# The first weights of a diffusion step's modulation ahead of the small rows, the second group in a buffer of its own, x behind the first activation

## The reference

```python
mod = (jax.nn.silu(c) @ w_mod[l] + b_mod[l])[:, None, :]      # c_ctx for the context tokens
shift1, scale1, gate1, shift2, scale2, gate2 = jnp.split(mod, 6, axis=-1)
mix, new_ctx = token_mixer(modulate(x, shift1, scale1), w_in, ...)   # attention and RG-LRU
x = layer_norm(ALPHA * x + gate1 * mix, ln1_g, ln1_b)
ff = expert_choice_ffn(modulate(x, shift2, scale2), w_router, w_gate_up, w_down)
x = layer_norm(ALPHA * x + gate2 * ff, ln2_g, ln2_b)
```

## Time and profile before

| | us |
|---|---|
| median of 3 runs | 944.03 (942.81 to 944.91) |
| the profiled execution, its own time | 944.97 |
| its span, first to last instruction | 943.20 |
| TensorE busy | 882.9 (94%) |
| VectorE busy | 774.0 (82%) |
| ScalarE busy | 576.1 (61%) |
| GpSimd busy | 160.8 (17%) |
| first modulation matmul starts | 12.88 |
| first `hmod` starts | 40.76 |

### The profile page before, as it was taken

The page is one execution under the profiler, slowest core; times in us unless marked ns, Lnnn a source line. Parts: engine busy times, 40 slices in busy tenths (PEclk is TensorE's granted clock), DMA queues, the critical chain, the costliest instruction groups (busy, mean ns, idle before and its releaser), DMA issues.

```text
span 943.2 us, 11657 instructions
## 1 busy us (share of the span) xinstructions
PE 882.9 (94%) x4643; PEld 602.8 (64%) x4643; DVE 774.0 (82%) x802; ACT 576.1 (61%) x588; POOL 160.8 (17%) x108
## 2 busy tenths in 40 slices
PE   2899999889999976999999999999999999999995
PEld 0389978356678843666666666666666666666663
DVE  2777736578779887888989989998998998998877
ACT  1344367735751343777777777777777777677653
POOL 1000300010011014203203303303302311320220
PEclk9899999999999986999999999999999999999999
DMA  8930500663048387999999999999999999999716
GB/s 281 396 129 1 207 1 1 262 162 114 1 152 314 138 322 286 362 419 386 415 393 385 417 389 392 410 396 391 401 403 387 390 409 382 384 414 388 275 15 200
DMA packets 57358, 272.81 MB, mean 289 GB/s; under 512 B 6788, under 2 KB 7032, under 8 KB 40920
## 3 DMA queue, kind: packets, MB, share of 16 engines
q1 hardware_dynamic: 48264, 242.76, 65.7%
q0 software_dynamic: 7600, 24.06, 9.2%
q10 hardware_dynamic: 1440, 5.24, 1.4%
HBM read 258.05 MB, written 14.00 MB: 288 GB/s over the span
## 4 chain that ended last, share of the span: by engine, by line
PE 85%; DMA 5%; DVE 5%; ACT 2%; issue 1%; SPq 1%; ACTq 0%; DVEq 0%
PE PS L918 24%; PE PS L920 24%; PE PS L919 24%; DMA ring<-in_w_mod 4%; PE PS L932 2%; PE PS L1081 2%; PE PS L1065 2%; PE PS L1035 1%; PE PS L1104 1%; PE PS L1223 1%; PE PS L1236 1%; DMA acc_scratch<-ysc,idx_u 1%; PE PS L1159 1%; DVE smin L1558 1%; ACT prob L721 1%
## 5 line engine op out<-in xcount | busy, mean ns | idle before, releaser
L1737 DVE TENSOR_TENSOR Wl<-wr,Wh 128x2048 fp32r<-128x2048 f32 x190 | 432.4, 2289 | 50.1 <-ACT Wh L832 50.1
L832 ACT ACTIVATE Wh<-wr 128x2048 fp32r<-128x2048 f32 x192 | 367.3, 1915 | 67.6 <-PE PS L920 67.6
L918 PE MATMUL PS<-Wh,Xh 128*80 128x512 f32 x512 | 202.4, 395 | 1.5 <-DVE Xl L1742 0.8
L920 PE MATMUL PS<-Wl,Xh 128*80 128x512 f32 x512 | 201.0, 393 | 0.0
L919 PE MATMUL PS<-Wh,Xl 128*80 128x512 f32 x512 | 200.8, 392 | 0.0
L543 POOL DMA_INDIRECT acc_scratch<-ysc,idx_u x15 | 81.2, 5410 | 418.6 <-DVE ysc L1768 418.6
L920 PEld LDWEIGHTS PS<-Wl,Xh 128*80 128x80 f32 x512 | 75.7, 148 | 42.1
L918 PEld LDWEIGHTS PS<-Wh,Xh 128*80 128x80 f32 x512 | 75.7, 148 | 41.8 <-issue 1.2
L918 PE MATMUL PS<-Wh,HTh 128*80 128x512 f32 x256 | 101.6, 397 | 0.0
L919 PEld LDWEIGHTS PS<-Wh,Xl 128*80 128x80 f32 x512 | 75.8, 148 | 39.4
L919 PE MATMUL PS<-Wh,HTl 128*80 128x512 f32 x256 | 100.4, 392 | 0.0
(11 more groups left out here) (298 smaller groups left out, 1211.4 us busy)
## 6 DMA issues: line engine op xcount, KB each, us to landing
wr<-in_w_gate_up SPq DMA_DIRECT2D x128, 1024.0 KB, 13.6
wr<-in_w_down SPq DMA_DIRECT2D x64, 1024.0 KB, 12.3
ring<-in_w_mod SPq DMA_DIRECT2D x24, 1024.0 KB, 9.0
xt<-in_x_sample ACTq DMA_DIRECT2D x8, 512.0 KB, 8.6
ring<-in_w_in SPq DMA_DIRECT2D x4, 1024.0 KB, 12.4
ring<-in_w_out SPq DMA_DIRECT2D x4, 1024.0 KB, 11.9
w_qkv<-in_w_in SPq DMA_DIRECT2D x4, 768.0 KB, 10.2
h_scratch<-h POOLq DMA_DIRECT2D x5, 512.0 KB, 5.8
```

Of the source, the lines that this page charges most:

```text
L832: act.activation(Wh[n % NWH][:], wr[s][:], ACT.Copy).then_inc(W_hi, 1)
L918: pe.matmul(out, w[0], x[0], start=first, stop=False)
L920: return pe.matmul(out, w[0], x[1], start=False, stop=last)
L1737: dve.tensor_tensor(Wl[s][:], wr[s][:], Wh[n % NWH][:].bitcast(F32), ALU.subtract).then_inc(W_lo, 1)
```

## The change

SyncE no longer issues the ten small requests: it starts with the four units of group 0, without a wait, then four requests for group 1, which go into a new buffer `w_mod1` (in the space that `Hh` and `Hl` take later) with semaphores of their own, then `w_qkv`, the router and the units of `w_in`, whose waits on `mod_used` are those of the ring's slots as before. The rows go to a tile of their own, `rows`. ScalarE issues the ten small requests, runs a Silu on a scratch element, which loads that table, waits for `nb_ok`, writes `cT`, and only then issues the five chunks of x. `x_again` is folded into `x_in` with a higher count, which changes no wait.

```diff
@block.sync
-        for r0, src in ((R_C, ...), ... (R_H0, ...)):
-            sp.dma_start(ring[r0:r0 + src.shape[0], 7, 0:P], src).then_inc(rows_in, 16)
-            if r0 == R_C:
-                sp.dma_start(consts[:], t["consts"][:, 0:P + 256]).then_inc(rows_in, 16)
...
-            if u == 3:
-                sp.wait_ge(rows_t, 1)
...
-        for u in range(8):
-            stream(u, slots(u), w_mod_v[:, 2 * (u % 4):2 * (u % 4) + 2, u // 4, :])
-            if u == 7:
-                for m in range(4):
-                    sp.dma_start(w_qkv[:, 2 * m:2 * m + 2, 0:QKV], w_in_v[:, 2 * m:2 * m + 2, 0:QKV]).then_inc(w_qkv_in[m], 16)
-                sp.dma_start(w_rt[:], rt_w).then_inc(misc_in, 16)
+        for u in range(4):
+            stream(u, slots(u), w_mod_v[:, 2 * u:2 * u + 2, 0, :])
+        for m in range(4):
+            sp.dma_start(w_mod1[:, 2 * m:2 * m + 2, :], w_mod_v[:, 2 * m:2 * m + 2, 1, :]).then_inc(mod1_in[m], 16)
+        for m in range(4):
+            sp.dma_start(w_qkv[:, 2 * m:2 * m + 2, 0:QKV], w_in_v[:, 2 * m:2 * m + 2, 0:QKV]).then_inc(w_qkv_in[m], 16)
+        sp.dma_start(w_rt[:], rt_w).then_inc(misc_in, 16)
@block.scalar
-        act.wait_ge(rows_in, 16 * 10)
+        for r0, src in ((R_C, ...), ... (R_H0, ...)):
+            act.dma_start(rows[r0:r0 + src.shape[0], :], src).then_inc(rows_in, 16)
+            if r0 == R_C:
+                act.dma_start(consts[:], t["consts"][:, 0:P + 256]).then_inc(rows_in, 16)
+
+        act.wait_ge(ct_zero, 1)
+        act.activation(table_scr[:, 1:2], epsc[:], ACT.Silu)
+        act.wait_ge(nb_ok, 1)
+        act.activation(cT[:, :, 0], cols[:, R_C:R_C + 8], ACT.Silu).then_inc(ct_ok, 1)
+        act.activation(cT[:, :, 32], cols[:, R_CTX:R_CTX + 8], ACT.Silu).then_inc(ct_ok, 1)
         for c in range(CH):
             src = x_s[:, c, :] if c < PC else t["x_prompt"][0]
             act.dma_start(xt[:, c, :], src).then_inc(x_in[c], 16)
-
-        act.wait_ge(nb_ok, 1)
-        act.wait_ge(ct_zero, 1)
-        act.activation(cT[:, :, 0], cols[:, R_C:R_C + 8], ACT.Silu).then_inc(ct_ok, 1)
-        act.activation(cT[:, :, 32], cols[:, R_CTX:R_CTX + 8], ACT.Silu).then_inc(ct_ok, 1)
         act.activation(nsp[:, 2, :], lscr[:, 0, :], ACT.Exp, scale=-1.0).then_inc(lam_e, 1)
@block.tensor
-        pe.transpose(bank(7, 0, R_END), ring[0:R_END, 7, 0:P], ident[0:R_END, 0:R_END]).then_inc(rows_t, 1)
+        pe.transpose(bank(7, 0, R_END), rows[0:R_END, :], ident[0:R_END, 0:R_END]).then_inc(rows_t, 1)
...
-                if k % 2 == 0:
+                if k % 2 == 0 and g == 1:
+                    pe.wait_ge(mod1_in[k // 2], 16)
+                elif k % 2 == 0:
                     landed_wait(pe, u0 + k // 2)
+                src = w_mod1 if g == 1 else ring
```

More of the change, by code:

```diff
@@ L186, in _build @@
     idx_u = tile("idx_u", [SL, NE], U32)
-    table_scr = tile("table_scr", [P, 1])
+    table_scr = tile("table_scr", [P, 2])
     epsc = tile("epsc", [P, 1])
@@ L214, in _build @@
     WX = [[at(f"WX{g}{h}", [P, KC, RG], Dz + 16384 * (2 * g + h), F32R) for h in range(2)] for g in range(2)]
+    w_mod1 = at("w_mod1", [P, KC, 1024], Ez)
     Hh = at("Hh", [P, KC, NT], Ez, F32R)
@@ L222, in _build @@
     Z = Fz + 19456
+    rows = at("rows", [P, P], Fz + 2048)
     m_rowA = [at("m_rowA0", [P, H2], Fz), at("m_rowA1", [P, H2], Fz + 4096)]
@@ L296, in _build @@
     x_in = [sem(f"x_in{c}") for c in range(CH)]
-    x_again = [sem(f"x_again{c}") for c in range(CH)]
+    mod1_in = [sem(f"mod1_in{m}") for m in range(4)]
     w_qkv_in = [sem(f"w_qkv_in{m}") for m in range(4)]
@@ L343, in landed_wait @@
         eng.wait_ge(landed[unit % 4], 16 * (unit // 4 + 1))
-    U_R, U_MB, U_O, U_G = 8, 12, 24, 28
+    U_R, U_MB, U_O, U_G = 4, 8, 20, 24
     block = ctx.enter_context(nc.Block())
@@ L603, in _ @@
     def _(act):
-        act.wait_ge(rows_in, 16 * 10)
+        bm_rows = t["b_mod"][0].rearrange("(r p) -> r p", p=P)
+        for r0, src in ((R_C, t["c"][0].rearrange("(r p) -> r p", p=P)),
+                        (R_CTX, t["c_ctx"].rearrange("(r p) -> r p", p=P)),
+                        (R_BM, bm_rows),
+                        (R_CW, t["conv_w"][0].rearrange("w (j p) -> (w j) p", p=P)),
+                        (R_CB, t["conv_b"][0].rearrange("(j p) -> j p", p=P)),
+                        (R_BA, t["b_rg_a"][0].rearrange("d (j p) -> (d j) p", p=P)),
+                        (R_BX, t["b_rg_x"][0].rearrange("d (j p) -> (d j) p", p=P)),
+                        (R_LAM, t["rg_lambda"][0].rearrange("d (j p) -> (d j) p", p=P)),
+                        (R_H0, t["state_h"][0, 0].rearrange("d (j p) -> (d j) p", p=P))):
+            act.dma_start(rows[r0:r0 + src.shape[0], :], src).then_inc(rows_in, 16)
[6 more added lines that the diff above has]
+        act.activation(cT[:, :, 32], cols[:, R_CTX:R_CTX + 8], ACT.Silu).then_inc(ct_ok, 1)
         for c in range(CH):
@@ L607, in _ @@
             act.dma_start(xt[:, c, :], src).then_inc(x_in[c], 16)
-        act.wait_ge(nb_ok, 1)
-        act.wait_ge(ct_zero, 1)
-        act.activation(cT[:, :, 0], cols[:, R_C:R_C + 8], ACT.Silu).then_inc(ct_ok, 1)
-        act.activation(cT[:, :, 32], cols[:, R_CTX:R_CTX + 8], ACT.Silu).then_inc(ct_ok, 1)
         act.activation(nsp[:, 2, :], lscr[:, 0, :], ACT.Exp, scale=-1.0).then_inc(lam_e, 1)
-        act.activation(table_scr[:], epsc[:], ACT.Sqrt)
+        act.activation(table_scr[:, 0:1], epsc[:], ACT.Sqrt)
         def split_w(k, src, w):
@@ L784, in _ @@
         act.wait_ge(rg_sum, RJ)
-        act.dma_start(xt[:, PC, :], t["x_prompt"][0]).then_inc(x_again[PC], 16)
+        act.dma_start(xt[:, PC, :], t["x_prompt"][0]).then_inc(x_in[PC], 16)
         cat_evac(N_PAIR - 1)
@@ L810, in _ @@
                 for again in range(PC):
-                    act.dma_start(xt[:, again, :], x_s[:, again, :]).then_inc(x_again[again], 16)
+                    act.dma_start(xt[:, again, :], x_s[:, again, :]).then_inc(x_in[again], 16)
             std(i, 1)
             if i == CH - 1:
-                act.activation(table_scr[:], epsc[:], ACT.Exp)
+                act.activation(table_scr[:, 0:1], epsc[:], ACT.Exp)
             act.wait_ge(y2_ok, i + 1)
@@ L854, in silu_gate @@
                 act.activation(gate_act[:, lo:hi], PS[0:SL, lo:hi], ACT.Silu).then_inc(act_ok, 1)
-        act.activation(table_scr[:], epsc[:], ACT.Silu)
+        act.activation(table_scr[:, 0:1], epsc[:], ACT.Silu)
         act.wait_ge(mod_used, 5 * KC + 2 * W_POOL)
@@ L928, in mod_group @@
             for k in ks:
-                if k % 2 == 0:
+                if k % 2 == 0 and g == 1:
+                    pe.wait_ge(mod1_in[k // 2], 16)
+                elif k % 2 == 0:
                     landed_wait(pe, u0 + k // 2)
+                src = w_mod1 if g == 1 else ring
                 for half in range(2):
                     last = pe.matmul(PS[MG * half:MG * half + MG, 512 * b:512 * b + 512], cT[:, k, :],
-                                     ring[:, k, 512 * half:512 * half + 512], start=(k == 0), stop=(k == KC - 1))
+                                     src[:, k, 512 * half:512 * half + 512], start=(k == 0), stop=(k == KC - 1))
                 last.then_inc(mod_used, 1)
@@ L951, in _ @@
         mod_group(0, 0)
-        mod_group(1, 4, range(0, 4))
+        mod_group(1, None, range(0, 4))
         pe.wait_ge(mrow_ok, 1)
         row_transposes(m_rowA[0], 1)
-        mod_group(1, 4, range(4, 8))
+        mod_group(1, None, range(4, 8))
         pe.wait_ge(xn_ok, CH)
@@ L1627, in residual @@
                     dve.wait_ge(g1_in[0 if c < PC else 1], 16)
-                    dve.wait_ge(x_again[c], 16)
+                    dve.wait_ge(x_in[c], 32)
                     if i >= 2:
```

## The result

The changed kernel takes 949.64 us (median of 4 runs, 949.3 to 951.67) against 944.33 us for the kernel before beside it: a ratio of 1.0063, 95% interval 1.0044 to 1.0082. It is slower by some 5 us. A second measurement gave 948.38 us, ratio 1.0048 (1.0032 to 1.0064). The forecast was 942.4, in a range of 940.4 to 947.5.

What follows compares the result with a forecast made beforehand. TensorE's chain bounds the kernel, so only the opening counts: `modT` at the later of 37.6 (weights) and 39.1 (x), against 40.72, saves 1.6 us from 944.03, giving 942.4 us, range 940.4 to 947.5.

Steps and rivals of the forecast that it cites:

- What bounds the kernel: Whole kernel: TensorE's chain bounds it, busy 882.9 of 943.2 us; what the opening wins or loses is passed on whole.
- The two-path rule: Opening: `modT` ends at the later of last weight landing + 3.56 us and last x landing + 10.99 us.
- Weights first: SyncE's opening: weights requested 3.77 us earlier, 3.1 us of it won (2.8 to 3.8); last unit lands at 34.1.
- The clog: Opening, 5 to 8 us: GpSimd's two repeated rows hold 78% of the DMA engines' time for 0.06 MB.
- Small rows on ScalarE's queue: Opening: rows land beside the weights, 2.5 us later than 6.44, at 9.0 (7.4 to 9.5).
- x behind the Silus: ScalarE's opening: x issued at 10.5, 4.1 us later, flight 17.6 us, landing at 28.1; `modT` ends at 39.1.
- The rows are held behind the weights: Rival, ScalarE's queue before the Silus: rows land at 13.4, x at 32.5, 2.8 us lost, 946.8 us; chance 0.25.
- the slower end of the same rival: Rival with rows held behind weights, x taking 19.6 us of flight instead: 948.8 us; rival's chance 0.25.
- price of 0.7 us a unit: Rival's term, DMA queues in the opening: each weight unit ahead delays the other queue 0.7 us; rival's chance 0.25.
- the even counts of the earlier trace: Both DMA queues, 12 to 16 us: 0.84 MB against 0.79, 214 and 211 packets, taken as turns of one packet.
- The weights stay the bound: Rival, opening: x lands at 26.5, `modT` ends at 37.6 by the weights, 3.1 us saved, 940.9 us; chance 0.25.

Runs made afterwards that it cites:

- the buffer half: The changed kernel with the ten small requests first on SyncE's queue again and x issued ahead of the Silus: 944.59 us, ratio 1.0011.
- the best version: The changed kernel with x issued before the Silus and GpSimd's repeated rows and `gtab` late: 939.32 us, ratio 0.9954.
- the run before it: The kernel before, with GpSimd's two repeated rows issued later and `gtab` made behind the loop it preceded: 941.03 us, ratio 0.9970.
- the run with one unit: The changed kernel, SyncE issuing one unit of w_mod and waiting for the small rows before the others: 942.97 us, ratio 1.0000.

## Why the prediction was wrong

**What bounds the kernel: right.** What the opening lost was passed on: the first `hmod` came 4.34 us late, the activation at 232 4.35 us, and the two spans differ by 947.5 - 943.2 = 4.3. In between the lateness was 5.90 us at the gates, so not everything stood as far from the first `hmod` as before; the granted clock, as read above, fits as the reason. The medians differ by 5.3 and, in the second measurement, by 4.1 us. The two-path rule held to a tenth: x landed at 34.11, and 34.11 + 10.99 = 45.10, where `modT` ended at 45.07.

**Weights first: half of it.** I had the last unit at 34.1; it landed at 35.66, 1.50 us earlier than before and not 3.1. The 3.77 us of earlier issue were real, and the buffer half by itself was worth nothing. The clog is not the reason for the shortfall: without it the order is worth 1.23 us (34.17 against 32.94), and the clog costs about 3 us in either order (37.16 against 34.17, and 35.89 against 32.94 with x early in both). The pipe did not use the earlier start to the full: queue 1, alone from 2 to 5, moved 0.92 MB, which is 0.31 MB per us against the 0.408 that I had counted with, and even without the clog the best version had moved only 0.83 MB more by 10 us than the run before it (277 against 194 GB/s), or 2.0 us of a full pipe. The rest of the difference stays open.

**Small rows on ScalarE's queue: this step failed.** It said 9.0, in 7.4 to 9.5; the rows landed at 15.45. I bounded the hold by what one unit had lost to the repeated rows, and left what the rows lose to the units to a rival. Measured: one unit ahead adds 2.3 us (9.07 against 6.74), the repeated rows 2.7 (15.45 against 12.77), and the remaining 3.7 of the 8.7 us (15.45 - 6.74) come with the other units. The parts overlap, and the same order gave landings up to 0.9 us apart, so this is a rough division.

**x behind the Silus: the path was right, its input wrong, and its size partly luck.** x took 34.11 - 16.71 = 17.4 us from issue to landing, where I had 17.6, and was issued 1.26 us behind the rows, where I had 1.5. Feed 15.45 into my own sum and it gives 15.45 + 1.5 + 17.6 + 11.0 = 45.55, against the measured 45.07. But I had taken 2.0 us off the 19.6 because the first packet had come 4.6 us after its issue and I laid that to the clog. With the clog long over, the first packet still came about 3.5 us after its issue: that delay is the turn behind the weights, and only some 1 us of the shorter flight came from it. The rest came later in the flight.

**The rivals.** "The rows are held behind the weights" is what happened, at 0.25. I had priced it at 946.8, with 13.4 for the rows; the slower end of the same rival, 948.8, was nearer to 948.4 and 949.6. Its price of 0.7 us a unit came from one row, the first packet of x 4.6 us after issue, and shared the delay among three units; the run with one unit shows that a single one costs 2.3 us. I then held the even counts of the earlier trace rows against the rival, and they were evidence on two streams in full flow, not on a small request that arrives while a megabyte is under way. The same showed exactly that arrival, and I read it as part of the clog. The kernel before has the proof: from 8 to 10 the clog was over, x had been issued since 6.44, and of the hardware queues only the weights' moved anything:

```profile
q1 hardware_dynamic: 132, 0.54, 75.1%
```

"The weights stay the bound" did not happen in the change, and does in the best version.

**The range** ended at 947.5 because I took the rival's own price as its end. It should have reached to its upper end, which stood in the text.

## What to carry to other kernels

Before moving small requests, on which an engine's first step waits, beside a stream of large ones, look in the trace for a request that arrived while a large one was under way, and take its delay, not the bandwidth, as the price: here 3.5 to 4.5 us to the first packet, each time a queue had stood still. Whatever is issued in program order behind the wait for them inherits it, and pays it once more: here 2.6 MB of x, issued behind an activation that it did not need, turned a delay that costs nothing (942.84 us) into 5 us. A slow little transfer (64 KB with a quarter KB repeated to each partition) is worth more looking at than the order of the big ones: taking it out of the opening gave 3 us in either order; the reordering gave 1.2 us of its own.

## What was not expected of the hardware

Two 32 KB requests that repeat one row to 128 partitions had 78% of the time of 16 engines, over 3 us in the kernel before and 2 us in the changed one. That is about 0.78 us for each of the 48 packets of GpSimd's queue in the earlier trace rows, worked out from the share, against 0.16 us for a packet of weights in the earlier trace rows. A single megabyte ahead kept another queue at no packet at all for 3 us, though two running queues share evenly. A megabyte cut into four requests of 32 partitions took until about 8 to move, in two of 128 partitions until about 5.7, as in one. Why the first turn is so long, and why the four requests are slower, stays open.
